# A norm's weight row spread over the partitions: products with one row of weights, or with 128 rows of which one is not zero

## The chip, the cores and the metric

The kernel runs on one core of a Trainium2 chip. The metric is the device time of one execution in microseconds. The kernel before took 1679.24 us, the median of 3 runs (1679.14 to 1679.53).

## What is computed

One inference step of a decoder trunk with one layer, for a prompt of 1024 tokens and for 8 samples of 8 tokens (64 rows), at a width of 1024. The layer begins with a norm and one large projection:

```python
def rms_norm(x, g):
    xf = x.astype(jnp.float32)
    y = xf * lax.rsqrt(jnp.mean(xf * xf, axis=-1, keepdims=True) + EPS)
    return (y * g.astype(jnp.float32)).astype(x.dtype)

h = rms_norm(x, g_pre_mix)
cb, cc, ch, q, k, v, ga, gb = jnp.split(h @ w_in, IN_SPLITS, axis=-1)
```

After that come a short gated convolution, stick-breaking attention, the output projection, a convolutional feed-forward part and an embedding gate, each with norms of its own. The change concerns only how `g_pre_mix`, the weight of the first norm (1024 values), gets onto all partitions.

## The kernel before, in words

The 1088 rows of x are held as nine blocks of at most 128 rows (`xn`, and `xlast` for the samples), with a row of x on a partition. Each block b goes through the same steps before the first projection can use it:

1. SyncE loads it (`x_start`, line 687). SyncE's order at the start is x blocks 0 and 1, the weights of job 0 (`raw`, line 655), x block 2, `g_mix` (the norm's weight, broadcast to 128 partitions by a DMA of 512 KB, line 683), x blocks 3 and 4, the weights of job 1, x blocks 5 to 8, the biases and the page table. Then it waits for the page table's landing before it loads keys, and it loads the weights of job 2 behind the first keys.
2. ScalarE squares it and sums (`x0_square`, line 1227), and takes a root as exp(-0.5 ln) (`x0_root`, lines 1232 and 1233).
3. VectorE improves the root by a Newton step (`x0_newton`, lines 1985 to 1991) and multiplies the block by the root and by the norm's weight (`x0_scaled`, line 2008).
4. TensorE transposes it in eight parts of 128x128 (`x0_turn`, through the helper `turned`, line 2794).
5. ScalarE writes the high part of the transposed block (`x0_high`, line 1240), VectorE the rest (`x0_low`, line 2016). Each product of the projection is made of three: high by high, low by high, high by low.

For a part of the weights (a "job") ScalarE makes the high part `wh` (`whi`, line 1196); for jobs 0 and 1 GpSimd subtracts it to get `wl` (line 1074), and VectorE passes the word on (`wlo_by_pool`); from job 2 on VectorE subtracts itself (line 1963).

The weight row in step 3 comes from two places. For blocks 2 to 8 it is `g_mix`, which the DMA has spread. For blocks 0 and 1 that DMA would be waited for, so the row is loaded alone (`grow`, one row of 4 KB, on ScalarE's queue, line 1217) and TensorE spreads it: a product of `ones`, one row of 128 ones that VectorE sets (line 1971), with `grow`, one row of 1024, into `pairs[0]` in two halves of 512 columns (line 2933; each fp32 product is two records in the trace). `x0_scaled` for blocks 0 and 1 waits for `p_mix`, the second product's count.

TensorE's order at the start is written out by hand in `pair` of the TensorE program (lines 2928 on). `idle(i)` issues filler transposes of the identity, `WARM = (8, 4, 11, 5, 6)` of them:

```python
idle(4)
pe.wait_ge(d_ones, 1)
pe.wait_ge(row_in, 16)
...
idle(0)
x0_turn(0)
idle(1)
x0_turn(1)
idle(2)
begin_job()
by_blocks()
```

`by_blocks` makes the first tile of 384 columns in two parts: the columns of block 0 (8 steps of three products, lines 2869 to 2871, with `x0_turn(2)` after the fourth step), then `idle(3)` and the columns of blocks 1 and 2. Then come the other tiles of jobs 0 and 1 with the turns of the later blocks between them (`in_tile`, lines 2840 to 2842), job 2, and the rest of the kernel.

GpSimd begins with the identity (lines 1042, 1043; TensorE waits for it before its first transpose), then makes masks and cleared tiles one after the other (lines 1046 to 1071), then `wl` of jobs 0 and 1. VectorE begins with `ones`, a small tile `xst` and two cleared halves of `kl` (lines 1971 to 1975) before the first Newton step.

Of the kernel before, what the change touches and what calls it, by code (L numbers as in the profile page):

```python
# [12 lines left out]
P = 128  # L13
D = 1024
# [178 lines left out]
def build(nc, inp, out, gate_spill, x1_spill, x2_spill, f_spill):  # L193
    with ExitStack() as ctx:
        def sem(name):
            return ctx.enter_context(nc.semaphore(name))
# [30 lines left out]
        a = Region(R1, R2)  # L227
# [8 lines left out]
        a = Region(R1, R2)  # L236
# [20 lines left out]
        a = Region(R3, RTOP)  # L257
# [23 lines left out]
        a = Region(R2 + ACTS, R3)  # L281
# [34 lines left out]
        aas, xs = a2.take("aas", [P, P]), a2.take("xs", [P, P])  # L316
        a = Region(start_at, start_at + 20480)
        xlast, g_mix = a.take("xlast", [P, D]), a.take("g_mix", [P, D])
        grow, ones = a.take("grow", [1, D]), a.take("ones", [1, P])
        junk0 = a.take("junk0", [P, 512]).bitcast(mybir.dt.bfloat16)  # L320
        xst = a.take("xst", [P, 48])
        farh = a.take("farh", [P, 2, NB, NT])
# [2 lines left out]
        a = Region(R3T, RTOP)  # L325
# [5 lines left out]
        a = Region(R3T, RTOP)  # L331
# [4 lines left out]
        a = Region(R3T, RTOP)  # L336
# [29 lines left out]
        a = Region(R3T, RTOP)  # L366
# [119 lines left out]
        g_const = sem("g_const")  # L486
# [18 lines left out]
        row_in, d_ones, p_mix = sem("row_in"), sem("d_ones"), sem("p_mix")  # L505
# [12 lines left out]
        a_gh = sem("a_gh")  # L518
        a_fold, d_fold, a_pack = sem("a_fold"), sem("d_fold"), sem("a_pack")
        a_sum, d_sum = sem("a_sum"), sem("g_wlo_d_sum")  # L520
        g_wlo, SUM0 = d_sum, 2

        d_lo = sem("d_lo")
        d_unit = sem("d_unit")
# [509 lines left out]
        def _(pool):  # L1034
            me = Count()

            def then(ins):
                ins.then_inc(g_self, 1)
                pool.wait_ge(g_self, me.step())

            g = nc.gpsimd
            then(g.memset(ident[:, :], 0.0))
            g.affine_select(out=ident[:, :], in_=ident[:, :], compare_op=ALU.not_equal, fill=1.0, base=0,
                            pattern=[[-1, P]], channel_multiplier=1).then_inc(g_const, 1)

            then(g.memset(far[:, :], 0.0))
            g.affine_select(out=far[:, :], in_=far[:, :], compare_op=ALU.is_gt, fill=-BIG, base=0,
                            pattern=[[-1, P]], channel_multiplier=1).then_inc(g_const, 1)
# [121 lines left out]
        def _(act):  # L1170
            s_ = nc.scalar
            me = Count()
            job, unit, mis = Count(), Count(), Count()
# [39 lines left out]
            def tables(name):  # L1213

                s_.preload_act_table_set(name)

            act.dma_start(grow[:, :], inp["g_pre_mix"]).then_inc(row_in, 16)
            tables("natural_log_exp_and_others")

            def x0(b):  # L1220
# [729 lines left out]
        def _(dve):  # L1950
            v = nc.vector
            me = Count()
            job, unit, xhn = Count(), Count(), Count()

            def then(ins):
                ins.then_inc(d_self, 1)
                dve.wait_ge(d_self, me.step())
# [10 lines left out]
                dve.wait_ge(p_unit, unit.step())  # L1968
                return unit_bank(u)[:, 0:GROUPS[gr][1]]

            v.memset(ones[:, :], 1.0).then_inc(d_ones, 1)
            then(v.memset(xst[:, :], 1.0))
            v.memset(xst[:, 40:41], EPS).then_inc(d_eps, 1)
            for h in range(2):
# [1 line left out]

            def wlo_by_pool():

                dve.wait_ge(g_wlo, job.step())
                dve.sem_inc(d_lo, 1)  # L1980

            def x0_newton(b, n):
# [765 lines left out]
        def _(pe):  # L2748
            t_ = nc.tensor
            job, unit, mis, att = Count(), Count(), Count(), Count()  # L2750
# [24 lines left out]
            def begin_job():  # L2775
                pe.wait_ge(d_lo, job.step())
# [21 lines left out]
            def x0_turn(b):  # L2798

                r = block_rows(b)  # L2800
                pe.wait_ge(d_x0, b + 1)
                if b >= 3:
                    pe.wait_ge(d_x0l, 2 * (b - (3 if b < 8 else 2) + 1))
                x = xn[:, b, :] if b < BLK else xlast[0:NS, :]
                for k in range(KD):
                    ins = turned(x0_pair(b)[:, k * P:k * P + r], x[:, k * P:(k + 1) * P], r)
                    if k % 4 == 3:
                        ins.then_inc(p_x0, 1)

            def pair(c):  # L2810
# [35 lines left out]
                def in_tile(j, gr, between={}):  # L2846
                    b = open_unit(j, gr)
                    for k in range(KD):
                        for what, n in between.get(k, ()):
                            what(n)  # L2850
                        step(b, j, gr, k)

                def idle(i):
                    for _ in range(WARM[i]):
                        turned(banks[1 if i in (2, 3) else 7][:, 0:P], ident[:, :])

                def by_blocks():

                    b = open_unit(0, 0)
                    for at_, end in ((0, P), (P, 3 * P)):  # L2860
                        if at_:
                            idle(3)
                        pe.wait_ge(d_x0l, 2 * (end // P))
                        o, cols = b[:, at_:end], slice(at_, end)
                        for k in range(KD):
                            if not at_ and k == KH:
                                x0_turn(2)
                            (h, l), xhi, xlo = tall(0, k), xh[:, k, cols], xl[:, k, cols]
                            t_.matmul(o, h, xhi, start=(k == 0), stop=False, skip_group_check=True)
                            t_.matmul(o, h, xlo, start=False, stop=False, skip_group_check=True)  # L2870
                            ins = t_.matmul(o, l, xhi, start=False, stop=(k == KD - 1), skip_group_check=True)
                    ins.then_inc(p_unit, 1)
# [8 lines left out]
                def conv_rows():  # L2881

                    b = once()
                    pe.wait_ge(cwr_in, cwn.step(32))
                    pe.sem_inc(pe_held, 1)
                    turned(b[:, 0:P], cwr[:, :]).then_inc(p_m, 1)
# [39 lines left out]

                if first:
                    idle(4)
                    pe.wait_ge(d_ones, 1)
                    pe.wait_ge(row_in, 16)  # L2930
                    for i in range(2):

                        ins = t_.matmul(banks[i], ones[:, :], grow[:, 512 * i:512 * i + 512], start=True, stop=True)
                    ins.then_inc(p_mix, 1)
# [8 lines that stand above are left out]
                    in_tile(1, 0, {1: [(x0_turn, 3)], 3: [(x0_turn, 4)], 5: [(x0_turn, 5)]})  # L2943
                    pe.wait_ge(d_x0l, 12)
                    conv_rows()
                    in_tile(0, 1, {6: [(x0_turn, 6)]})
                    past(0)
                    in_tile(1, 1, {1: [(x0_turn, 7)], 3: [(x0_turn, 8)]})
                    pe.wait_ge(d_x0l, 2 * NBK)
                    past(1)  # L2950
                    in_tile(0, 2)
                    in_tile(1, 2, {4: [(pages, 0), (past, 2)]})
                else:
                    conv_rows()
                    begin_job()
                    for gr in range(NG):
                        in_tile(0, gr)
                    past(0)
                    begin_job()
                    in_tile(1, 0)  # L2960
                    past(1)
                    in_tile(1, 1)
                    in_tile(1, 2, {4: [(pages, 0), (past, 2)]})
# [534 lines left out]
```

## Time and profile before

| | before |
|---|---|
| median of 3 runs | 1679.24 us |
| the profiled execution's own time | 1680.04 us |
| its span (first to last instruction) | 1678.3 us |
| TensorE matmul busy | 1667.5 us, 99% |
| VectorE busy | 1101.4 us, 66% |
| ScalarE busy | 794.6 us, 47% |
| GpSimd busy | 321.0 us, 19% |
| TensorE in the chain that ended last | 94% |

The profile is of one execution; its times count from the first instruction. "Busy" is the share of the span in which an engine had an instruction in work. The chain is followed back from the last instruction, at each step to what released it. PE is TensorE's matmul, PEld its weight load, DVE VectorE, ACT ScalarE, POOL GpSimd, SP SyncE; a q behind a name means the engine's instruction queue. Instructions are named by their line in the kernel.

### The profile page before, as it was taken

What the parts mean: (1) busy time and instruction counts of PE and PEld (TensorE: products, weight loads), DVE (VectorE), ACT (ScalarE), POOL (GpSimd) and SP (SyncE); (2) the same over time, 40 slices, a digit from 0 to 9 for tenths busy, and PEclk for the clock granted to TensorE, in tenths of its full rate; (3) what the DMA queues carried; (4) which work ended last, traced back from release to release, by engine and by line L of the source; (5) the groups of instructions that cost most, each with busy time, mean ns of one, the idle gap of its engine ahead of it and who ended that gap; (6) DMA issues with size and microseconds to landing.
All of it is one profiled execution on the core that took longest, in us unless ns stands there. A gap on an engine that the chain in (4) does not pass through costs nothing.

```text
span 1678.3 us, 27174 instructions
## 1 busy us (share of the span) xinstructions
PE 1667.5 (99%) x9101; PEld 1462.9 (87%) x9101; DVE 1101.4 (66%) x1606; ACT 794.6 (47%) x1391; POOL 321.0 (19%) x268
## 2 busy tenths in 40 slices
PE   9999999999999999999999999999999999999998
PEld 8999998999999999988888888888888878888886
DVE  7365246325533646547688888888888688776576
ACT  7345344444534453125454444444444444465675
POOL 2000000000000000002346666666664000000000
PEclk9999999999999999999999999999999999999999
DMA  5312221132123114443132222222222852245333
GB/s 182 97 55 74 80 77 55 57 99 68 60 67 92 53 63 149 151 169 116 68 97 80 79 79 79 79 72 72 79 79 97 293 191 80 90 150 186 112 123 118
DMA packets 176598, 170.64 MB, mean 102 GB/s; under 512 B 16207, under 2 KB 144555, under 8 KB 176492
## 3 DMA queue, kind: packets, MB, share of 16 engines
q1 hardware_dynamic: 165546, 164.41, 30.5%
q10 hardware_dynamic: 10946, 4.91, 1.0%
q8 instruction: 55, 0.90, 0.2%
q14 instruction: 51, 0.42, 0.1%
HBM read 129.66 MB, written 39.62 MB: 101 GB/s over the span
## 4 chain that ended last, share of the span: by engine, by line
PE 94%; DVE 3%; DMA 1%; issue 1%; SPq 1%; ACT 0%; DVEq 0%; POOL 0%; POOLq 0%; ACTq 0%
PE pair L3152 11%; PE pair L2840 9%; PE pair L2842 9%; PE pair L2841 9%; PE pair L3212 8%; PE pair L3214 8%; PE pair L3213 8%; PE pair L2794 6%; PE pair L3368 3%; PE pair L3370 3%; PE pair L3369 3%; PE pair L3221 3%; PE pair L3021 2%; PE pair L2771 2%; PE pair L2769 2%; PE pair L2770 2%
## 5 line engine op out<-in xcount | busy, mean ns | idle before, releaser
L2840 PE MATMUL pair<-xh,wh 128*128 128x384 f32 (+1 forms) x952 | 324.4, 341 | 0.0
L2842 PE MATMUL pair<-xh,wl 128*128 128x384 f32 (+1 forms) x952 | 311.3, 327 | 0.0
L2841 PE MATMUL pair<-xl,wh 128*128 128x384 f32 (+1 forms) x952 | 310.8, 326 | 0.0
L2840 PEld LDWEIGHTS pair<-xh,wh 128*128 128x128 f32 x952 | 179.3, 188 | 5.4 <-issue 4.0
L2841 PEld LDWEIGHTS pair<-xl,wh 128*128 128x128 f32 x952 | 179.4, 188 | 0.0
L2842 PEld LDWEIGHTS pair<-xh,wl 128*128 128x128 f32 x952 | 178.8, 188 | 0.0
L1074 POOL TENSOR_TENSOR srow<-hn,hn 128x512 f32<-128x512 f32 x8 | 12.0, 1506 | 791.1 <-DVE hn L2322 790.8
L3368 PE MATMUL pair<-woph,foph 128*128 128x512 f32 x308 | 120.9, 393 | 0.1
L3370 PE MATMUL pair<-woph,fopl 128*128 128x512 f32 x308 | 120.0, 390 | 0.0
L3369 PE MATMUL pair<-wopl,foph 128*128 128x512 f32 x308 | 120.0, 390 | 0.0
L1408 ACT ACTIVATE keep<-pair,bias 128x512 f32<-128x512 f32 (+4 forms) x100 | 58.2, 582 | 115.6 <-DVE pair L2175 71.5
L1963 DVE TENSOR_TENSOR wl<-raw,wh 128x1024 fp32r<-128x1024 f32 x46 | 56.3, 1225 | 73.9 <-ACT wh L1196 73.4
L1764 ACT ACTIVATE foph<-f 128x512 fp32r<-128x512 f32 x77 | 48.3, 628 | 71.7 <-PE pair L3370 68.3
L2175 DVE TENSOR_TENSOR pair<-pair,far 128x128 f32<-128x128 f32 x64 | 16.3, 296 | 81.7 <-PE pair L2996 59.6
L3368 PEld LDWEIGHTS pair<-woph,foph 128*128 128x128 f32 x308 | 57.8, 188 | 13.8 <-issue 1.3
L3370 PEld LDWEIGHTS pair<-woph,fopl 128*128 128x128 f32 x308 | 57.8, 188 | 12.1
L3369 PEld LDWEIGHTS pair<-wopl,foph 128*128 128x128 f32 x308 | 57.9, 188 | 11.7
L3212 PE MATMUL pair<-bh,tch 128*128 128x512 f32 x168 | 67.4, 401 | 0.0
L3214 PE MATMUL pair<-bh,tcl 128*128 128x512 f32 x168 | 65.7, 391 | 0.0
L3213 PE MATMUL pair<-bl,tch 128*128 128x512 f32 x168 | 65.5, 390 | 0.0
L3212 PE MATMUL pair<-bh,adh 128*128 128x512 f32 x168 | 65.5, 390 | 0.0
L3214 PE MATMUL pair<-bh,adl 128*128 128x512 f32 x168 | 65.4, 389 | 0.0
(417 smaller groups left out, 4289.5 us busy)
## 6 DMA issues: line engine op xcount, KB each, us to landing
rawp<-in_w_up SPq DMA_DIRECT2D x88, 256.0 KB, 3.8
raw<-in_w_in SPq DMA_DIRECT2D x80, 256.0 KB, 3.2
wd<-in_w_down SPq DMA_DIRECT2D x55, 256.0 KB, 3.0
f_spill<-cv SPq DMA_DIRECT2D x22, 552.0 KB, 2.8
f<-f_spill SPq DMA_DIRECT2D x44, 256.0 KB, 5.6
gat<-gate_spill SPq DMA_DIRECT2D x16, 544.0 KB, 4.5
x_spill<-x SPq DMA_DIRECT2D x16, 512.0 KB, 3.0
gate_spill<-stg SPq DMA_DIRECT2D x32, 192.0 KB, 1.9
```

Source lines behind the costliest of these rows:

```text
L1408: s_.activation(keep[n % 2][:, 4 * P - w:4 * P], b, ACT.Sigmoid, scale=-SCALE, bias=bias2[:, h + 2:h + 3] if n != SAMPLE else bias2[:, 5:6 ...
L2794: return t_.transpose(b, src, ident[0:rows, 0:rows])
L2840: t_.matmul(b, h, xhi, start=(k == 0), stop=False, skip_group_check=True)
L2841: t_.matmul(b, h, xlo, start=False, stop=False, skip_group_check=True)
L2842: ins = t_.matmul(b, l, xhi, start=False, stop=(k == KD - 1), skip_group_check=True)
L3152: ins = t_.matmul(o[:, 512 * c:512 * c + 512], x, w(t, c), start=first and i == 0, stop=last and i == 2, skip_group_check=True)
L3212: t_.matmul(o, w, x, start=n in "1675" and k == 0, stop=False, skip_group_check=True)
L3213: t_.matmul(o, w, xlow, start=False, stop=False, skip_group_check=True)
L3214: ins = t_.matmul(o, wlow, x, start=False, stop=k == KH - 1, skip_group_check=True)
L3368: t_.matmul(o, xh_[:, cols], w[0][:, :], start=n in (0, 2, 3, 5) and k == 0, stop=False, skip_group_check=True)
L3369: t_.matmul(o, xh_[:, cols], w[1][:, :], start=False, stop=False, skip_group_check=True)
L3370: ins = t_.matmul(o, xl_[:, cols], w[0][:, :], start=False, stop=k == KF - 1, skip_group_check=True)
```

## The change

`grow` and `ones` become tiles of 128 rows. The DMA fills 32 rows of `grow`, each with the same 1024 weights (128 KB instead of 4 KB); GpSimd clears rows 32 to 63, between the identity and its next mask, and VectorE rows 64 to 127. Of `ones` all rows are cleared and row 0 is set to one. The product is thus the same sum, with 127 terms of zero. TensorE waits for VectorE's second count and for GpSimd's, as well as for the DMA. GpSimd's count is the first of a semaphore that also counts `wl` of jobs 0 and 1 and, at the kernel's end, two sums, so these counts move up by one.

```diff
-        grow, ones = a.take("grow", [1, D]), a.take("ones", [1, P])
+        grow, ones = a.take("grow", [P, D]), a.take("ones", [P, P])
...
-        g_wlo, SUM0 = d_sum, 2
+        g_grow, SUM0 = d_sum, 3
+        g_wlo, WLO0 = d_sum, 1
...
             g.affine_select(out=ident[:, :], in_=ident[:, :], compare_op=ALU.not_equal, fill=1.0, base=0,
                             pattern=[[-1, P]], channel_multiplier=1).then_inc(g_const, 1)
 
+            pool.wait_ge(g_const, 1)
+            g.memset(grow[32:64, :], 0.0).then_inc(g_grow, 1)
+            pool.wait_ge(g_grow, 1)
             then(g.memset(far[:, :], 0.0))
...
-            act.dma_start(grow[:, :], inp["g_pre_mix"]).then_inc(row_in, 16)
+            act.dma_start(grow[0:32, :], inp["g_pre_mix"].rearrange("l d -> (l d)").partition_broadcast(32)).then_inc(row_in, 16)
             tables("natural_log_exp_and_others")
...
-            v.memset(ones[:, :], 1.0).then_inc(d_ones, 1)
+            then(v.memset(ones[:, :], 0.0))
+            v.memset(ones[0:1, :], 1.0).then_inc(d_ones, 1)
+            v.memset(grow[64:P, :], 0.0).then_inc(d_ones, 1)
             then(v.memset(xst[:, :], 1.0))
...
-                dve.wait_ge(g_wlo, job.step())
+                dve.wait_ge(g_wlo, WLO0 + job.step())
...
                     idle(4)
-                    pe.wait_ge(d_ones, 1)
+                    pe.wait_ge(d_ones, 2)
+                    pe.wait_ge(g_grow, 1)
                     pe.wait_ge(row_in, 16)
```

## Rows read from the trace of the kernel before

**Rows 1.** The page: shares of the chain that ended last, by engine
```profile
...
PE 94%; DVE 3%; DMA 1%; issue 1%; SPq 1%; ACT 0%; DVEq 0%; POOL 0%; POOLq 0%; ACTq 0%
...
```

**Rows 2.** The chain in order of time, 0 to 60 us: start us, us, what
```profile
...
1.60 1.54 PE pair L2794 x6
3.14 3.71 PE pair L2933 x4
6.85 7.05 PE pair L2794 x39
...
```

**Rows 3.** Source line L2794 (transposes) in two windows: duration ns min/median/max, first and last start
```profile
...
L2794 PE MATMUL pair<-ident x7: 421/421/475, 6.8 to 8.1; 128*128 128x128 f32 x7
...
L2794 PE MATMUL pair<-ident x10: 272/272/273, 12.5 to 13.5; 128*128 128x128 f32 x10
L2794 PE MATMUL pair<-ident,xn x3: 272/273/317, 12.2 to 12.4; 128*128 128x128 f32 x3
...
```

**Rows 4.** Timeline of the entry: start us, us, engine line op out<-in; weight loads of the products
```profile
...
4.09 0.33 PEld L2933 LDWEIGHTS pair<-grow,ones 1*128 1x128 f32 x1 [0.52 <-issue]
...
4.94 0.33 PEld L2933 LDWEIGHTS pair<-grow,ones 1*128 1x128 f32 x1 [0.52 <-issue]
...
```

**Rows 5.** The same timeline, from x block 0 to the weights of job 1
```profile
...
4.63 1.06 ACT L1227 ACTIVATE junk<-xn 128x1024 bf16<-128x1024 f32 x1 [1.96 <-DMA xn<-in_x_prompt]
...
6.37 0.15 DVE L1985 TENSOR_SCALAR xst<-xst 128x1 f32<-128x1 f32 x1 [2.78 <-ACT xst L1233]
...
6.87 0.16 DVE L1991 SCALAR_TENSOR_TENSOR xst<-xst 128x1 f32<-128x1 f32 x1
7.06 1.28 DVE L2008 SCALAR_TENSOR_TENSOR xn<-xn,xst,pair 128x1024 f32<-128x1024 f32 x1
...
8.95 1.28 DVE L2008 SCALAR_TENSOR_TENSOR xn<-xn,xst,pair 128x1024 f32<-128x1024 f32 x1
9.07 2.38 POOL L1074 TENSOR_TENSOR wl<-raw,wh 128x1024 fp32r<-128x1024 f32 x1 [1.00 <-ACT wh L1196]
9.21 1.06 ACT L1227 ACTIVATE junk<-xn 128x1024 bf16<-128x1024 f32 x1 [0.23 <-DMA xn<-in_x_prompt]
...
10.40 1.09 ACT L1240 ACTIVATE xh<-pair 128x512 fp32r<-128x512 f32 x2
...
11.03 1.29 DVE L2016 TENSOR_TENSOR xl<-pair,xh 128x512 fp32r<-128x512 f32 x2 [0.80 <-ACT xh L1240]
...
12.92 1.28 DVE L2008 SCALAR_TENSOR_TENSOR xn<-xn,xst,g_mix 128x1024 f32<-128x1024 f32 x1
...
13.66 0.31 PE L2869 MATMUL pair<-xh,wh 128*128 128x128 f32 x1
...
15.04 1.06 PE L2794 MATMUL pair<-ident,xn 128*128 128x128 f32 x8
15.70 1.08 ACT L1240 ACTIVATE xh<-pair 128x512 fp32r<-128x512 f32 x2 [0.76 <-PE pair L2794]
...
17.80 2.40 POOL L1074 TENSOR_TENSOR wl<-raw,wh 128x1024 fp32r<-128x1024 f32 x1 [6.35 <-ACT wh L1196]
...
```

**Rows 6.** SyncE's longest wait before 80 us, and the loads by stretch (last column GB/s)
```profile
...
SPq L643 <- DMA pgt<-in_page_table: 8.3, 1, 8.3
...
4.00:18.50 14.50, 14.50 (x86) 12.34 (x85) 10.02 (x21) 12.32 (x25) 6.67 (x17) 1.00 1.05 368
...
```

**Rows 7.** Timeline around the first use of the weights of job 2
```profile
...
46.37 1.21 DVE L1963 TENSOR_TENSOR wl<-raw,wh 128x1024 fp32r<-128x1024 f32 x1
...
49.15 0.34 PE L2840 MATMUL pair<-xh,wh 128*128 128x384 f32 x1
...
```

**Rows 8.** GpSimd's memsets, groups by line, engine and form
```profile
...
L1070 POOL MEMSET qpad<- 128x1152 f32 x1 | 1.1, 1057 | 0.0
...
```

**Rows 9.** TensorE and its granted clock (PEclk is the third figure) at the end of the span
```profile
...
1671.60:1674.50 2.90, 0.00 (x0) 1.00 0.01 3
1674.50:1678.30 3.80, 0.00 (x0) 0.50 0.37 138
...
```

## The prediction

> **What bounds the kernel now.** I read the page first: TensorE is busy nearly throughout, and the chain that ended last is 94% TensorE [rows 1]. The change touches only the entry, so the question is narrow: by how much does it move the moment from which TensorE works without a break, and is anything later tied to an absolute time? The chain in order of time answers for the entry [rows 2]: transposes and four one-row products follow each other on TensorE until 13.9 us, then the chain passes through ScalarE, VectorE and back while the first blocks of x are normed, turned and split. From 30 us on it is TensorE nearly alone.
>
> The second thing to see is TensorE's own pace. The page's clock line reads 9 from the first slice, but before 12.2 us it has no record of the clock; the instructions tell more. Transposes of 128x128 start 213 ns apart at 7 us (x7, first to last 6.8 to 8.1) and 109 ns apart at 13 us (x10, 12.5 to 13.5), with 421 and 272 ns for one [rows 3]. That factor of two is the step from 1.2 to 2.4 GHz, and it falls at 12.2 us, where a 317 ns transpose stands between both kinds [rows 3]. TensorE had had no gap since 1.60 [rows 2]. So it ran 10.6 us at the low clock though it was always occupied. In the first part of that time it did six transposes, then four products with one active row (the form 1*128, 3.14 to 6.85), and from then on only transposes with 128 rows [rows 2, 4]. The likeliest reading: products with one active row don't raise the clock, and the rise came 12.2 - 6.85, about 5.4 us, after the last of them. The change makes exactly these four full-height.
>
> **The change, part by part.**
> The products. Still two fp32 products of 512 columns in four records, the last ones 0.85 us apart (loads at 4.09 and 4.94 [rows 4]), which is 4 x 213 ns for 4 x 128 columns: the pace goes by columns, the same for 1 row [rows 4] and 128 rows [rows 3]. So 128 rows cost nothing per se. No column is added.
>
> The clock. Now all TensorE work from 1.60 on has 128 rows. If the rise keeps the distance that it had to the end of the one-row work, it comes at 1.60 + 5.4 = 7.0 us; it may come earlier, while the products run, which would then end up to 1.7 us sooner (four at 0.43 instead of 0.85). Where it falls between 5 and 10 us makes no difference to what follows, as (a) and (b) show.
>
> What that gives, step by step, with warm transposes at 0.109 instead of 0.213 us. (a) The spread weight row is wanted by the first scaling (L2008) at 7.06, right behind VectorE's own Newton steps, whose last ends at 6.87 + 0.16 = 7.03 [rows 5]; the products end at 6.85. An earlier row is worth nothing there: late next are the Newton steps, behind ScalarE and the landing of x block 0. (b) x0_turn(0) follows the end of the scaling, 8.34, and takes 0.9 instead of 1.7 us, but ScalarE can't take it before 10.40, when it is through with the square of block 2, whose block landed at 9.21 [rows 5]. Nothing again. (c) x0_turn(1), the 11 filler transposes and the first product at 13.66 [rows 5]: warm, turn 1 would begin when scaling 1 is done, 8.95 + 1.28 = 10.23, end at 11.2, the fillers end at 12.4, and the first product would wait for xl of block 0, ready at 11.03 + 1.29 = 12.32. So it starts 1.2 us earlier. (d) Twelve products later TensorE needs block 2 scaled. That ends at 12.92 + 1.28 = 14.20, while turn 2 started at 15.04 [rows 5]. The path takes 15.04 - 14.20 less 0.05 to 0.2 of hand-over: **0.65 to 0.8 us saved**, and the other 0.4 of the 1.2 becomes a new wait of TensorE for VectorE at about 14. (e) Behind that, the next steps hang on turn 2: ScalarE's split at 15.70 waited for TensorE; VectorE's split and TensorE's second part follow it, and so do the weights of job 1, whose low part GpSimd makes from 17.80 to 20.20 when ScalarE has made the high one [rows 5]. They all shift together, so the gain is kept. I also looked for something fixed in time that would eat it. SyncE waits 8.3 us for the page table's DMA [rows 6] and loads keys and the weights of job 2 behind that, but VectorE has split those at 46.37 + 1.21 = 47.6 and TensorE's tile with them begins at 49.15 [rows 7]: 1.5 us of slack, beside a gain below 1. From there to the end TensorE is the bound, and a gain at the entry arrives whole.
>
> The larger DMA. One row of 4 KB becomes 32 rows, 128 KB, on ScalarE's queue at 0.81, beside SyncE's first block of x. All loads from 4 to 18.5 us run at 368 GB/s [rows 6], which is their limit here. The added 127 KB are 0.34 us of that, so every later landing moves by 0 (if they fit in before the stream is full) to 0.34 us. x block 0 (4.63) and block 2 (9.21) are both waits for a landing and both on the path of (d) [rows 5]. I take the upper end, since the copy shares its first microsecond with block 0: **0.34 lost**. The row itself must be there when TensorE is through with its six transposes at 3.14 [rows 2]. I expect 2.5 to 3.6 us, from block 0's own 128 rows of 4 KB, which took until 4.6; at worst the products end 0.5 later, 7.3 cold, 0.3 behind the Newton steps, which would add to the 0.34 only if the clock stays low.
>
> GpSimd. One memset of 32x1024. A memset of 1152 columns took it 1057 ns [rows 8], so about 0.95 us for 1024, if the time goes by columns, and with the waits before and behind it 1.2 us. It starts when the mask is done that also releases TensorE at 1.60 [rows 2] and ends near 1.6 + 0.1 + 0.95 = 2.65, before 3.14. Everything behind it on GpSimd comes 1.2 us later: the last of its constants ended at 9.07 - 1.00 = 8.07 [rows 5], now 9.3; then wl of job 0, before at 9.07, starts 0.2 late and ends at 11.7, wanted by TensorE at 12.4 at the earliest. Cover is 0.7 us; without it the 0.2 would count.
>
> VectorE. Two small memsets and a self wait in place of one, and 64x1024 of zeros: by GpSimd's rate again 0.95, in all 1.3 us more. Begun near 0.9 that ends near 2.5, before TensorE asks. What follows on VectorE ends 1.3 late, and it was idle for 2.78 us before 6.37 [rows 5]. Nothing. The added waits on TensorE stand in front of the products alone. Renumbered counts cost nothing, and no tile moves, since a one-row tile took 4096 bytes of each partition before as well.
>
> **Sum:** -0.75 + 0.34 = -0.4 us (ends: -0.8 and -0.35 with the clock early). The profiled execution lasted 1680.04, of which 1678.3 are the span; 0.4 less is 1679.64. The median of the three runs is 0.80 below that execution, which puts the forecast at 1679.24 - 0.4 = **1678.8**. It is 0.02%; a measurement of this kernel tells about 0.2% (3.4 us) from no change, so this is "the same".
>
> **The rivals.**
> (1) Clock unmoved. The 127 added rows are zeros, and the one-row form may not be the reason for the late rise. For it: only one rise is recorded, so the cause is inferred. Against: the transposes that did precede the rise read the identity, 127 zeros of 128. Then only the DMA's 0.34 is left: 1679.6. Worked through the cold path, the weight row may come at 7.3 and add 0.3: 1679.9.
> The Trainium skill, "TensorE: Matmul & The Clock Gate", Part 1, lets sustained busy time open the gate and does not mention active rows. By it this rival would hold; the trace speaks against it, with 10.6 us of unbroken work at the low clock.
>
> (2) Slower: the clock rises early and falls again. With the products over by 5.9 and the 8 fillers warm, TensorE rests from about 6.8 to 8.7, where before it had no gap, and again near 10. If the clock falls there and the next rise comes 5.4 us after the rest, it is near 14: turn 0 from 8.7, fillers and turn 1 cold until 13.0, four more fillers cold, seven warm, end at 14.6 against 13.63 before. That is +0.95: 1680.2. Only if it stays cold past turn 2 (to about 18.5 us) does it add 1.7 for the fillers, up to 1.0 for twelve products and 0.8 for turn 2: 1682.7, and this is the point from which "slower" would begin. Against: the one fall that is recorded came near 1674.5, when TensorE had done nothing since at least 1671.6, 2.9 us [rows 9], and the rests here are below 2 us.
> [...]
>
> (3) The row or the loads come much later than thought (over 1 us): 1680.3, as each us of landing is a us on the path.
>
> **Numbers.** Early clock as forecast 0.62; rival 1 0.20; rival 2 0.12 (of it 0.02 beyond 3.4 us); rival 3 and unforeseen things 0.06. Three runs spread over 0.4 us and one profiled execution stood 0.8 above them, so I widen the ends: 1677.9 takes in the full 0.8 gain with half a us of scatter, 1680.3 takes in rivals 1 and the mild form of 2. Faster by over 0.2% would need 3.4 us, more than TensorE's entire loss to the low clock on the path: 0.01. Slower 0.03, same 0.96.
>
> **What would show it.** Transposes 109 ns apart already in x0_turn(0) or (1) and a record of the clock that begins before 8 us; gaps on TensorE at 7 to 8.4 and about 10; first product near 12.7; turn 2 near 14.7; everything after it 0.4 earlier. The landing of block 0 at 4.9 and of block 2 at 9.5 would show the DMA's price. Transposes still 213 ns apart at 11 us would mean rival 1, a return to 213 after 109 rival 2.

## The result, and the profile after

The changed kernel takes 1681.98 us in the median of 22 runs (1680.45 to 1682.66), the kernel before 1679.42 in 22 runs beside them (1678.73 to 1680.31). The medians are 2.6 us apart. The ratio of the runs is 1.0013, with a 95% interval of 1.0008 to 1.0019: slower, and outside the forecast's range of 1677.9 to 1680.3. It is less than the 0.2% that the text took as the bound of what can be told; with 22 runs of each it can be told. (Of all runs told of here one, of e7, took 1830.12 us in a slow state of the chip; it is left out of e7's median.)

The page of the changed kernel: the span, the busy time and the chain's shares, which stand against 1678.3 us and the 94% of [rows 1].

```profile
span 1680.1 us, 27177 instructions
...
PE 1665.8 (99%) x9101; PEld 1461.0 (87%) x9101; DVE 1104.3 (66%) x1608; ACT 795.0 (47%) x1391; POOL 321.2 (19%) x269
...
PE 93%; DVE 4%; SPq 1%; DMA 1%; issue 1%; ACT 0%; DVEq 0%; ACTq 0%
...
```

TensorE is busy 1.7 us less and the span is 1.8 us longer. So TensorE stands idle 3.5 us more than before, and its work in the entry takes less time, because more of it runs at the high clock. The timeline of the entry shows where (start us, us, engine line); it answers to [rows 2, 4, 5], with line numbers shifted by the change (2933 is now 2940, 2008 is 2014, 1991 is 1997).

```profile
...
1.61 0.94 POOL L1048 MEMSET grow<- 32x1024 f32 x1
...
4.71 3.75 PE L2940 MATMUL pair<-grow,ones 128*128 128x512 f32 x4 [1.57 <-DMA grow<-in_g_pre_mix]
...
5.30 1.06 ACT L1231 ACTIVATE junk<-xn 128x1024 bf16<-128x1024 f32 x1 [2.74 <-DMA xn<-in_x_prompt]
...
8.59 1.28 DVE L2014 SCALAR_TENSOR_TENSOR xn<-xn,xst,pair 128x1024 f32<-128x1024 f32 x1 [0.90 <-PE pair L2940]
...
9.61 1.06 ACT L1231 ACTIVATE junk<-xn 128x1024 bf16<-128x1024 f32 x1
9.64 2.37 POOL L1078 TENSOR_TENSOR wl<-raw,wh 128x1024 fp32r<-128x1024 f32 x1 [0.43 <-ACT wh L1200]
...
9.97 0.27 DVE L1993 TENSOR_SCALAR xst<-xst 128x1 f32<-128x1 f32 x1
10.28 1.74 DVE L1997 SCALAR_TENSOR_TENSOR xst<-xst 128x1 f32<-128x1 f32 x1
...
12.05 1.28 DVE L2014 SCALAR_TENSOR_TENSOR xn<-xn,xst,pair 128x1024 f32<-128x1024 f32 x1
...
13.39 1.10 PE L2800 MATMUL pair<-ident,xn 128*128 128x128 f32 x8 [1.89 <-DVE xn L2014]
...
15.44 0.30 PE L2875 MATMUL pair<-xh,wh 128*128 128x128 f32 x1
...
16.82 1.06 PE L2800 MATMUL pair<-ident,xn 128*128 128x128 f32 x8
...
```

The waits of the first 40 us name the two new ones (us in total, times, longest):

```profile
...
PE pair L2940 <- DMA grow<-in_g_pre_mix: 1.6, 1, 1.6
...
DVE xn L2014 <- PE pair L2940: 0.9, 1, 0.9
...
```

Read from the top. GpSimd's memset took 0.94 us, as forecast. TensorE was through with its six transposes at 3.14 as before, but the products start at 4.71, not 3.14: the copy of 32 rows landed only then. Block 0 of x landed at 5.30, not 4.63. The first scaling starts at 8.59 instead of 7.06, after 0.9 us of waiting for the products. So far the delay is 1.5 us. Then comes something that the forecast had not seen: VectorE's last Newton step for block 1, an instruction on 128x1 elements that takes 0.16 us, takes **1.74 us**. It starts at 10.28, while GpSimd's subtraction for job 0 runs from 9.64 to 12.01, and it ends when that ends. In the kernel before, the same step ran at 8.75, GpSimd began at 9.07 [rows 5], and the second scaling at 8.95. The step for block 3, though, was held in that kernel too, inside GpSimd's second subtraction. Both stand in the timeline of the kernel before:

```profile
...
8.75 0.16 DVE L1991 SCALAR_TENSOR_TENSOR xst<-xst 128x1 f32<-128x1 f32 x1
...
18.02 2.21 DVE L1991 SCALAR_TENSOR_TENSOR xst<-xst 128x1 f32<-128x1 f32 x1
...
```

In the change the second scaling starts at 12.05, 3.1 us late, and turn 1 at 13.39 instead of 11.1.

Part of it is taken back, because turn 1 now runs wholly at the high clock: 1.10 us instead of 1.60. The transposes by duration (min/median/max ns, first and last start), which answer to [rows 3]:

```profile
...
L2800 PE MATMUL pair<-ident x12: 272/421/421, 8.3 to 11.2; 128*128 128x128 f32 x12
...
L2800 PE MATMUL pair<-ident,xn x8: 272/272/338, 10.0 to 10.8; 128*128 128x128 f32 x8
...
```

The step from 421 to 272 ns falls at about 10.1, where a 338 ns transpose opens turn 0, against 12.2 before. Turn 1 at 13.39 lies behind either. The eleven fillers behind turn 1 take 1.36 us in both kernels. The first product starts at 15.44 (13.66 before) and turn 2 at 16.82 (15.04 before): **+1.78 us**. From there these two executions stay together: the last product starts at 1672.97 against 1671.24, +1.73, and their times, 1681.77 and 1680.04, differ by 1.73.

### The profile page after: what moved, and what is told of

It is laid out like the page before. It is cut to its first block, busy times and chain, and to the rows that moved or that the text cites. A ratio compares the mean times of both kernels' runs of the same rounds, so it can differ in the third digit from the quotient of the medians.

```text
span 1680.1 us, 27177 instructions
## 1 busy us (share of the span) xinstructions
PE 1665.8 (99%) x9101; PEld 1461.0 (87%) x9101; DVE 1104.3 (66%) x1608; ACT 795.0 (47%) x1391; POOL 321.2 (19%) x269
## 4 chain that ended last, share of the span: by engine, by line
PE 93%; DVE 4%; SPq 1%; DMA 1%; issue 1%; ACT 0%; DVEq 0%; ACTq 0%
PE pair L3159 11%; PE pair L2846 9%; PE pair L2848 9%; PE pair L2847 9%; PE pair L3219 8%; PE pair L3221 8%; PE pair L3220 8%; PE pair L2800 5%; PE pair L3375 3%; PE pair L3376 3%; PE pair L3377 3%; PE pair L3228 3%; PE pair L3028 2%; PE pair L2777 2%; PE pair L2775 2%; PE pair L2776 2%
## 5 line engine op out<-in xcount | busy, mean ns | idle before, releaser
L3377 PEld LDWEIGHTS pair<-woph,fopl 128*128 128x128 f32 x308 | 57.8, 188 | 12.2
```

The source lines that it names most:

```text
L3377: ins = t_.matmul(o, xl_[:, cols], w[0][:, :], start=False, stop=k == KF - 1, skip_group_check=True)
```

## The experiments

Each experiment is told as a difference from the kernel before or from the change. The time beside each is the median of 11 runs (22 for the change), and that of the kernel before over the runs made beside them (22 to 35). The landmark is the start of turn 2 in the profiled execution. From there to the end ten of the thirteen profiled executions took 1664.9 to 1665.3 us. The others took 1663.9 (e6), 1663.6 (e11) and 1666.1 (e8). In e6 and e8 most of that difference is TensorE's idle time between 1200 and 1400 us, 0.1 and 1.7 us against 0.8 before; why it differs was not looked into, nor e11's. The products start at 3.07 in the timeline, which counts them from the first record, and at 3.14 in the chain [rows 2].

| kernel | median us | before us | 95% interval of the ratio | products start | turn 2 starts |
|---|---|---|---|---|---|
| before | | | | 3.07 | 15.04 |
| the change | 1681.98 | 1679.42 | 1.0008 to 1.0019 | 4.71 | 16.82 |
| e1, only the copy to 32 rows | 1681.82 | 1679.61 | 1.0006 to 1.0024 | 4.67 | 16.78 |
| e2, 128 rows, copy of one row after clearing | 1681.83 | 1679.61 | 1.0004 to 1.0022 | 6.61 | 17.13 |
| e3, change, subtraction after the Newton steps | 1680.35 | 1679.61 | 0.9995 to 1.0013 | 4.71 | 15.23 |
| e4, change, GpSimd clears nothing | 1681.99 | 1679.61 | 1.0006 to 1.0024 | 4.66 | 16.77 |
| e6, before, one filler more | 1679.84 | 1679.59 | 0.9992 to 1.0010 | 3.29 | 14.39 |
| e7, before, four fillers more | 1681.29 | 1679.59 | 1.0005 to 1.0022 | 3.93 | 16.21 |
| e8, change, copy to 64 rows | 1683.38 | 1679.59 | 1.0012 to 1.0029 | 6.44 | 17.67 |
| e10, before, 128-row products on zeros | 1679.08 | 1679.59 | 0.9991 to 1.0008 | 2.94 | 14.24 |
| e12, before, an extra copy behind the row's | 1680.17 | 1679.63 | 0.9995 to 1.0013 | 3.07 | 15.24 |
| e9, before, job 1's low part by VectorE | 1678.34 | 1679.63 | 0.9984 to 1.0002 | 3.08 | 14.37 |
| e11, change, with e3's and e9's edits | 1679.21 | 1679.63 | 0.9990 to 1.0008 | 4.80 | 15.03 |

The theory: the copy of 32 rows lands late, and that lateness pushes a VectorE step behind GpSimd's subtraction, where it is held. The text calls this the cliff: a small delay is free, a little more sets off a large one. The rivals: the later landings of x alone (A), harm by the early clock (B), GpSimd's own delay (C), a delay that passes through one to one (D).

### The copy alone (e1)

```diff
-        grow, ones = a.take("grow", [1, D]), a.take("ones", [1, P])
+        grow, ones = a.take("grow", [P, D]), a.take("ones", [1, P])
...
-            act.dma_start(grow[:, :], inp["g_pre_mix"]).then_inc(row_in, 16)
+            act.dma_start(grow[0:32, :], inp["g_pre_mix"].rearrange("l d -> (l d)").partition_broadcast(32)).then_inc(row_in, 16)
...
-                        ins = t_.matmul(banks[i], ones[:, :], grow[:, 512 * i:512 * i + 512], start=True, stop=True)
+                        ins = t_.matmul(banks[i], ones[:, :], grow[0:1, 512 * i:512 * i + 512], start=True, stop=True)
```

> The kernel before with one part of the change: the DMA brings the weight row to 32 partitions, and the products still read one row. Theory (the copy of 32 rows lands late, and the delay makes VectorE's last Newton step of block 1 wait behind GpSimd's subtraction for job 0): the copy lands near 4.7 us, the products run 4.7 to 8.4, the first scaling ends near 9.9, the Newton step of block 1 takes about 1.7 us instead of 0.16, and turn 2 starts at 16.8 to 17.5 (15.04 before). Time 1.8 to 2.7 us above before. The clock rises later than in the kernel before, near 13.8, if one-row products don't raise it. Rival A (the loads of x are what counts, 0.34 to 0.7 us each): time 0.3 to 0.7 above before, turn 2 near 15.6. Rival B (the early clock of the change is what harms): time as before, within 0.3.

The timeline of e1: the products, the first scaling, the subtraction, the held step, turn 2.

```profile
...
4.67 3.75 PE L2933 MATMUL pair<-grow,ones 1*128 1x512 f32 x4 [1.53 <-DMA grow<-in_g_pre_mix]
...
8.55 1.28 DVE L2008 SCALAR_TENSOR_TENSOR xn<-xn,xst,pair 128x1024 f32<-128x1024 f32 x1 [0.89 <-PE pair L2933]
...
9.61 2.37 POOL L1074 TENSOR_TENSOR wl<-raw,wh 128x1024 fp32r<-128x1024 f32 x1 [1.53 <-ACT wh L1196]
...
10.24 1.75 DVE L1991 SCALAR_TENSOR_TENSOR xst<-xst 128x1 f32<-128x1 f32 x1
...
16.78 1.06 PE L2794 MATMUL pair<-ident,xn 128*128 128x128 f32 x8
...
```

The time is 2.2 us above before, and turn 2 starts within 0.04 of the change's. As far as the intervals tell, the copy alone makes the whole loss; the 128-row form, the memsets and the added waits make no difference that shows. Rivals A and B, as the whole cause, fall with the same run. One point of the expectation was missed: the clock rose at about 11.1, not 13.8, though the one-row products ended at 8.35 here.

### GpSimd's memset (e4)

```diff
...
-            pool.wait_ge(g_const, 1)
-            g.memset(grow[32:64, :], 0.0).then_inc(g_grow, 1)
-            pool.wait_ge(g_grow, 1)
...
-            v.memset(grow[64:P, :], 0.0).then_inc(d_ones, 1)
+            v.memset(grow[64:P, :], 0.0)
+            v.memset(grow[32:64, :], 0.0).then_inc(d_ones, 1)
...
-                    pe.wait_ge(g_grow, 1)
```

> The change with GpSimd's memset moved to VectorE, which clears rows 32 to 63 behind rows 64 to 127. Theory: GpSimd's constants end 1.2 us earlier, but its subtraction waits for ScalarE at 9.6 either way, and VectorE is done before the copy of 32 rows lands at 4.7: time within 0.3 us of the change's, turn 2 at 16.8. Rival C (GpSimd's delay is what costs): 1 us or more below the change's.

The time is 1681.99, and turn 2 starts at 16.77. Rival C falls: GpSimd's subtraction starts at 9.60 here and at 9.64 in the change, since both wait for ScalarE's high part.

### The hold taken away (e3)

```diff
                 pool.wait_ge(a_hi, j + 1)
+                if j == 0:
+                    pool.wait_ge(d_self, 8)
```

The count `d_self` reaches 8 when VectorE is through with the Newton steps of block 1.

> The change as it is, with one wait more: GpSimd starts its subtraction for job 0 only when VectorE is through with the Newton steps of block 1. Theory: that last step takes 0.16 instead of 1.74 us, the second scaling starts near 10.5 instead of 12.05, turn 2 starts at 15.0 to 15.4 instead of 16.82, and the time is 1.4 to 1.8 us below the change's, near before. Rival A (late loads and the late row alone make the 1.8 us): no more than 0.3 below the change's.

```profile
...
10.28 0.16 DVE L1999 SCALAR_TENSOR_TENSOR xst<-xst 128x1 f32<-128x1 f32 x1
10.47 1.28 DVE L2016 SCALAR_TENSOR_TENSOR xn<-xn,xst,pair 128x1024 f32<-128x1024 f32 x1
...
10.59 2.38 POOL L1078 TENSOR_TENSOR wl<-raw,wh 128x1024 fp32r<-128x1024 f32 x1 [1.40 <-DVE xst L1999]
...
15.23 1.06 PE L2802 MATMUL pair<-ident,xn 128*128 128x128 f32 x8
...
```

The step takes 0.16 again and the second scaling follows at 10.47. One wait **added** to GpSimd, which now starts its subtraction 0.95 later, brings turn 2 from 16.82 to 15.23 and the time from 1681.98 to 1680.35. The products start as late as in the change. Turn 2 is within 0.19 of the profiled execution of before, but that one had a late clock. Against e6 and e9, which have the rows and the copy of the kernel before and a clock that rose near 10.7 and 10.6 (turn 2 at 14.39 and 14.37), e3's turn 2 is still 0.85 late. So the held step is 1.6 us of the loss, and the rest, below 1 us, is something else (see "The base").

### A late row without any change to a DMA (e6, e7)

```diff
-WARM = (8, 4, 11, 5, 6)
+WARM = (8, 4, 11, 5, 7)
```

and the same with 10 in place of 7: fillers ahead of the one-row products.

> The kernel before with 7 filler transposes instead of 6 ahead of the one-row products; the DMA is as before. It makes the spread row 0.2 us later and nothing else. Theory (a cliff: the Newton step of block 1 must start before GpSimd's subtraction at 9.07, it had 0.3 us to spare): the step starts near 8.8 to 8.9 and takes 0.16; turn 2 within 0.2 of 15.04, the time as before within 0.3.

```profile
...
8.88 0.16 DVE L1991 SCALAR_TENSOR_TENSOR xst<-xst 128x1 f32<-128x1 f32 x1
8.96 2.38 POOL L1074 TENSOR_TENSOR wl<-raw,wh 128x1024 fp32r<-128x1024 f32 x1 [0.89 <-ACT wh L1196]
...
14.39 1.06 PE L2794 MATMUL pair<-ident,xn 128*128 128x128 f32 x8
...
```

> The kernel before with 10 fillers instead of 6: the spread row comes 0.85 us later (near 7.7), with no change to any DMA and with one-row products. Theory (the cliff): the Newton step of block 1 starts near 9.5, behind GpSimd's start at 9.07, and is held until 11.45, so the second scaling starts near 11.5 instead of 8.95 (2.5 later for a row 0.85 later), turn 2 starts at 16.0 to 16.4, the time is 1.0 to 1.4 above before. Rival A (the landings of x are what counts) and rival D (a delay passes through one to one): turn 2 at most 0.85 later, time at most 0.85 above before, the Newton step 0.16.

```profile
...
9.04 2.36 POOL L1074 TENSOR_TENSOR wl<-raw,wh 128x1024 fp32r<-128x1024 f32 x1 [0.94 <-ACT wh L1196]
...
9.52 1.89 DVE L1991 SCALAR_TENSOR_TENSOR xst<-xst 128x1 f32<-128x1 f32 x1
...
11.45 1.28 DVE L2008 SCALAR_TENSOR_TENSOR xn<-xn,xst,pair 128x1024 f32<-128x1024 f32 x1
...
16.21 1.06 PE L2794 MATMUL pair<-ident,xn 128*128 128x128 f32 x8
...
```

With one filler more the step starts at 8.88, GpSimd at 8.96, and the step takes 0.16. With four more it starts at 9.52, behind GpSimd's 9.04, and takes 1.89. A row later by 0.85 us makes the second scaling 2.5 us later (11.45 against 8.95) and turn 2 1.2 us later than in the profiled execution of before (1.8 later than in e6). The time is 1.7 above before, more than the 1.0 to 1.4 that was expected. That is the cliff, made without touching a copy or a product. Rivals A and D fall as the whole cause. (Turn 2 of e6 is even earlier than before, at 14.39 instead of the expected 15.04: its clock rose near 10.7; see below.)

### Later loads with the row on time (e12)

```diff
-            hold(page_in, 16)
+            hold(page_in, 32)
...
             act.dma_start(grow[:, :], inp["g_pre_mix"]).then_inc(row_in, 16)
+            act.dma_start(pv[0:32, 0:8, :].rearrange("p a b -> p (a b)"), inp["g_pre_mix"].rearrange("l d -> (l d)").partition_broadcast(32)).then_inc(page_in, 16)
```

The added copy counts on the semaphore for which SyncE waits before it loads keys, so that wait goes from 16 to 32.

> The kernel before with its one-row copy first on ScalarE's queue and a second copy of 32 rows behind it, into a tile that nobody reads (it is added traffic only). The row is on time, the loads of x are delayed as in the change. Theory (it is the row's lateness that trips the cliff, not x's): block 0 lands near 5.2 (4.6 before), the products still end near 6.85, the Newton step of block 1 takes 0.16, turn 2 starts at 15.0 to 15.6 (less if the clock rises before 11), time 0 to 0.6 above before. Rival A (x's delay is what costs): 1.5 or more above before.

```profile
...
5.06 1.06 ACT L1228 ACTIVATE junk<-xn 128x1024 bf16<-128x1024 f32 x1 [2.01 <-DMA xn<-in_x_prompt]
...
9.40 0.16 DVE L1992 SCALAR_TENSOR_TENSOR xst<-xst 128x1 f32<-128x1 f32 x1
...
10.06 2.37 POOL L1074 TENSOR_TENSOR wl<-raw,wh 128x1024 fp32r<-128x1024 f32 x1 [1.99 <-ACT wh L1196]
...
15.24 0.86 PEld L2795 LDWEIGHTS pair<-ident,xn 128*128 128x128 f32 x8 [0.40 <-DVE xn L2009]
...
```

Block 0 landed at 5.06, and the Newton step at 9.40 is not held, because the same later loads also delay GpSimd, to 10.06. Turn 2 starts at 15.24, and the time is 0.5 above before, which the interval doesn't tell from nothing. The clock rose near 10.0 here, with one-row products. Against e6 and e9, which have a like clock, turn 2 is 0.85 later: the later loads move it, through block 2's scaling, for which TensorE waits. So the traffic has a price of its own, below 1 us; it is the row's own lateness that trips the cliff.

### How late a copy lands (e8, e2)

e8 is the change with `grow[0:64]` and a broadcast to 64 in the copy, and GpSimd's memset left out.

> The change with the suspected cost doubled: the DMA brings the row to 64 rows (256 KB), GpSimd clears nothing. Theory (the copy competes with the first block of x and both land later in proportion): the copy lands near 5.5 us (4.7 with 32 rows), block 0 near 5.8 (5.3), turn 2 near 17.2, time 0.3 to 0.8 above the change's. Because GpSimd holds VectorE until 12.0 in any case, the 0.8 of the row comes through only in part. If the copy's price is a fixed one: 4.7 and the change's time.

The products in e8 (ns min/median/max, first and last start), and TensorE's wait for the copy (us, times):

```profile
...
L2936 PE MATMUL pair<-grow,ones x4: 967/1061/1192, 6.4 to 9.1; 128*128 128x512 f32 x4
...
  DMA grow<-in_g_pre_mix: 3.3, 1
...
```

The timeline of e8, for block 0 and the held step:

```profile
...
5.32 1.06 ACT L1228 ACTIVATE junk<-xn 128x1024 bf16<-128x1024 f32 x1 [2.61 <-DMA xn<-in_x_prompt]
...
11.92 0.96 DVE L1994 SCALAR_TENSOR_TENSOR xst<-xst 128x1 f32<-128x1 f32 x1
...
```

With 32 rows more the products start 1.7 us later (6.44 against 4.71), twice what was expected, and the time is 1.4 above the change's, where 0.3 to 0.8 was expected. Block 0 of x did not land later than in the change (5.32 against 5.30), so the theory of a delay in proportion for both failed. The step was held for a shorter time, since the row came so late that GpSimd was well into its subtraction.

e2 has the change's products, but VectorE clears the whole tile first and the copy brings one row. GpSimd's memset and TensorE's wait for it are left out, as in e4:

```diff
...
-            act.dma_start(grow[0:32, :], inp["g_pre_mix"].rearrange("l d -> (l d)").partition_broadcast(32)).then_inc(row_in, 16)
+            act.wait_ge(d_ones, 1)
+            act.dma_start(grow[0:1, :], inp["g_pre_mix"]).then_inc(row_in, 16)
...
+            v.memset(grow[:, :], 0.0).then_inc(d_ones, 1)
             then(v.memset(ones[:, :], 0.0))
             v.memset(ones[0:1, :], 1.0).then_inc(d_ones, 1)
-            v.memset(grow[64:P, :], 0.0).then_inc(d_ones, 1)
```

> The change with its DMA undone: VectorE clears the whole tile of 128 rows first (one memset), then the DMA brings one row of 4 KB; the products have 128 rows. Nothing is cleared by GpSimd. Theory: the row lands near 3.4 us, the products follow at once, the clock rises before 10 us, the Newton step of block 1 ends before GpSimd's subtraction begins (9.07) if the first scaling starts before 7.3, and turn 2 starts at 14.4 to 14.9. Time 0.2 to 0.7 us below before. If the first scaling starts later than 7.3, the Newton step is held and turn 2 comes after 16: time 1 to 1.5 above before. Rival B (an early clock falls again or harms): time above before by 1 or more although the Newton step isn't held. Rival A: as before within 0.2.

```profile
...
2.04 0.53 ACTq L1219 DMA_DIRECT2D grow<-in_g_pre_mix  x1
...
4.57 1.06 ACT L1229 ACTIVATE junk<-xn 128x1024 bf16<-128x1024 f32 x1 [0.67 <-DMA xn<-in_x_prompt]
...
6.61 3.75 PE L2937 MATMUL pair<-grow,ones 128*128 128x512 f32 x4 [3.47 <-DMA grow<-in_g_pre_mix]
...
8.98 2.36 POOL L1075 TENSOR_TENSOR wl<-raw,wh 128x1024 fp32r<-128x1024 f32 x1 [0.89 <-ACT wh L1197]
...
12.18 0.16 DVE L1995 SCALAR_TENSOR_TENSOR xst<-xst 128x1 f32<-128x1 f32 x1
...
```

This was meant to be the better version, and it failed on a term that I had taken for granted. A copy of 4 KB issued at 2.04 let the products start only at 6.61, 4.6 us later; the same copy issued at 0.81 let them start at 3.07, when TensorE was free. x's block 0 landed at 4.57 as ever. What differs is the moment: at 0.81 nothing is in flight, at 2.04 SyncE's loads of x are ahead of it. That these loads are the reason is the likeliest reading; no run separates it from another. The time is 2.2 above before, and not by the cliff. The expectation had the Newton step held if the row came late; here the row was so late that the step, at 12.18, came behind the whole of GpSimd's subtraction (8.98 to 11.34) and took 0.16. The row's own delay of 3.5 us is what moved turn 2 to 17.13.

### The clock alone (e10)

```diff
...
-            act.dma_start(grow[:, :], inp["g_pre_mix"]).then_inc(row_in, 16)
+            act.dma_start(pv[0:1, 0:8, :].rearrange("p a b -> p (a b)"), inp["g_pre_mix"]).then_inc(row_in, 16)
...
-            v.memset(ones[:, :], 1.0).then_inc(d_ones, 1)
+            then(v.memset(ones[:, :], 0.0))
+            v.memset(ones[0:1, :], 1.0).then_inc(d_ones, 1)
+            v.memset(grow[:, :], 0.0).then_inc(d_ones, 1)
...
-                    pe.wait_ge(d_ones, 1)
+                    pe.wait_ge(d_ones, 2)
```

> The products with 128 rows at the time they had before: they read a cleared tile of 128 rows, so the norm's weight is left out for blocks 0 and 1 (it comes out as zero); the row's DMA of 4 KB stays, into a tile that isn't used. TensorE works without a gap from 1.6 us, always with 128 rows. It tests the clock alone. Theory (one-row products don't raise the clock, 128-row ones do): the clock rises by 7.0, the products end by 6.9 or sooner, turn 2 starts at 14.3 to 14.5, the time is 0.5 to 0.8 below before. If the one-row form is not the reason: the clock rises near 12 as before, turn 2 at 15.04. If it falls again in the rests at 7 and 10: turn 2 after 15.

```profile
...
1.60 1.54 PE L2796 MATMUL pair<-ident 128*128 128x128 f32 x6 [1.60 <-POOL ident L1043]
2.94 2.58 PE L2935 MATMUL pair<-grow,ones 128*128 128x512 f32 x4
5.36 1.04 PE L2796 MATMUL pair<-ident 128*128 128x128 f32 x8
...
14.24 0.86 PEld L2796 LDWEIGHTS pair<-ident,xn 128*128 128x128 f32 x8 [0.41 <-DVE xn L2010]
...
```

The product records of e10 (ns min/median/max, first and last start):

```profile
...
L2935 PE MATMUL pair<-grow,ones x4: 592/732/1061, 2.9 to 4.9; 128*128 128x512 f32 x4
...
```

The four products take 2.58 us instead of 3.78, and the eight fillers from 5.36 on are at the high clock (8 in 1.04 us). The second product record, started at 3.8, lasts 871 ns, between the 1061 of the first and the 592 or 593 of the last two, so the rise falls between 3.8 and 4.5. It is one execution, but in none of the six profiled ones with one-row products did the clock rise before 10.0. TensorE rested from 6.4 to 8.5 after that and its clock did not fall back (turn 0, from 8.49, takes 1.09 us). Turn 2 starts at 14.24, 0.80 before the profiled execution of before. The medians differ by 0.5 us, which the interval doesn't tell from nothing.

### The other hold taken away (e9, e11)

Before and after alike, VectorE's Newton step of block 3 is held by GpSimd's second subtraction (2.21 us at 18.02 before, for 0.16 us of work). e9 lets VectorE make that low part itself:

```diff
-        g_wlo, SUM0 = d_sum, 2
+        g_wlo, SUM0 = d_sum, 1
...
-            for j in range(2):
+            for j in range(1):
                 pool.wait_ge(a_hi, j + 1)
...
                     x0_scaled(3, 1, 4)
-                    wlo_by_pool()
+                    wlo()
```

> The kernel before, with the low part of the weights of job 1 made by VectorE (1.22 us) right behind the third scaling, where GpSimd made it (2.4 us) and held VectorE's Newton step of block 3 for 2.21 us meanwhile. Theory (what GpSimd holds is on the path): the Newton step takes 0.16, block 3 is scaled by 19.6 instead of 21.5, the 0.26 us wait of TensorE at 21.6 and the 0.7 us one at 28.9 vanish, time 0.5 to 1.0 below before. If the hold is off the path: time as before, within 0.3.

VectorE in e9, and turn 2:

```profile
...
17.39 0.16 DVE L1991 SCALAR_TENSOR_TENSOR xst<-xst 128x1 f32<-128x1 f32 x1
...
18.78 1.22 DVE L1963 TENSOR_TENSOR wl<-raw,wh 128x1024 fp32r<-128x1024 f32 x1
...
14.37 0.86 PEld L2794 LDWEIGHTS pair<-ident,xn 128*128 128x128 f32 x8
...
```

The step takes 0.16 and the subtraction 1.22. Block 3 is scaled by 18.9. Of TensorE's two waits that were to vanish, the first is gone and the second is down from 0.7 to 0.3 us. 1678.34 is the lowest median of all kernels here, 1.3 below before, but the interval of the ratio (0.9984 to 1.0002) includes no change: that e9 is faster is likely and not shown.

> The change with the wait of e3 (GpSimd's subtraction for job 0 behind the Newton steps of block 1) and with the low part of job 1 made by VectorE. Theory: the two savings add: 1.4 to 1.8 and 0.5 to 1.0 below the change's, about 0.5 below before, and about as fast as the kernel before with only the second.

The time is 1679.21, 2.8 below the change and 0.4 below before. With both holds gone the change costs 0.9 against e9, which has the old products and the old copy; the expectation had them about equal. So no version that was run shows a gain by the 128-row product with its copy.

## Why the prediction was wrong, point by point

**The product's cost.** Right: 128 rows take as long as one. The last records are 0.85 us apart in both forms, and turn 2 starts at 16.78 in e1 and at 16.82 in the change.

**The landing of the row: the first step that failed.** "I expect 2.5 to 3.6 us ... at worst the products end 0.5 later." The products could start only at 4.7, and they ended 1.6 later. I had priced the copy by its bytes in a full stream (0.34 us), and its landing by a guess next to block 0's. In this place 31 rows more cost 1.6 us of waiting (4.71 against 3.07), and 32 more on top of them 1.7 (e8).

**x's landings.** Mis-sized: block 0 came 0.67 later, not 0.34 (5.30 against 4.63). In e12, where the loads alone are late, turn 2 is 0.85 later than in e6 and e9, and the median 0.5 above before, which its interval doesn't tell from nothing.

**How a delay goes on: the step that decided.** The text let each delay of the row pass through one to one, in the DMA's part ("0.3 behind the Newton steps, which would add to the 0.34") and in rival 3 ("each us of landing is a us on the path"). Rival 3 had the place, and 0.06 for itself together with everything unforeseen; it had no mechanism. What the runs show is a threshold: the Newton step of block 1 ran at 8.75, 0.3 us before GpSimd's subtraction at 9.07. A row 0.2 later costs nothing that shows (e6), one 0.85 later costs 1.7 us (e7), and the change loses 1.6 us of its 2.6 to that one held instruction (e3). The warning stood in the same trace: the same line took 2.21 us at 18.02, inside GpSimd's second subtraction. I took that stretch as steps of which "They all shift together" and did not ask which other overlap it could make.

The Trainium skill, "SBUF — State Buffer", section "Who interferes with whom", has the rule: a VectorE instruction with two inputs in SBUF and a GpSimd instruction that reads SBUF exclude each other, and the one that starts first keeps the other out to its end. The trace agrees: the steps with one tensor input ran beside the subtraction at their usual length (0.27 us at 9.97), the step with two inputs, 0.16 us by itself, took 1.74.

**The clock.** Half right. The rise did come earlier, 10.1 instead of 12.2, but not by 7.0. TensorE stood still from 3.14 to 4.71; whether that is why, no run shows. Nor does the 10.1 show that the rows did it: with the change's products it came between 8.0 (e11) and 10.7 (e2), with one-row products between 10.0 (e12) and 12.2 (before). Only e10, at 3.8 to 4.5, stands clear of both. That the rise keeps a distance of 5.4 us to the end of the one-row work was no rule: it came 5.4 us after their end in the kernel before, 3.2 after it in e12 and 2.7 after it in e1. And its worth was overrated. In the change it decides nothing: e1, with a rise 1.0 later, has the same turn 2, because the held scaling comes later than either. Even alone and earliest (e10), it gives 0.80 at turn 2 against the one profiled execution of before, but only 0.15 against e6 and e9, which have one-row products and a turn 2 at 14.39 and 14.37.

**What is late next.** Right as far as it went: with an early clock and the row on time, turn 2 starts right behind a wait for block 2's scaling (e10, e12).

**GpSimd's and VectorE's memsets.** Right: they take 0.94 and 0.91 us and are hidden, as e4 shows for GpSimd's.

**The base.** The change costs 1.73 between the two profiled executions and 2.56 between the medians. Up to turn 2, e9 is the kernel before, and yet its turn 2 came at 14.37 where the profile of before had 15.04, with a clock that rose near 10.6 instead of 12.2. So the profile that I worked from had a late rise, and lay 0.62 above its median (1680.04 against 1679.42); the change's lay 0.21 below its own. These two make up the other 0.83. The saving of 0.65 to 0.8 us in step (d) was taken from that late rise, and e6 and e9 had most of it with the old products and the old copy. Measured against their turn 2, the change is 2.4 us late, near the 2.6 of the medians. Of that the held step is 1.6 (e3). The other 0.85 remains in e3; the late row and the late loads share it, and no run divides it, though e12 shows that the loads alone can make as much. That the rise moves about from one execution to the next is seen in the profiles; its share in the medians was not measured.

**Rivals 1 and 2.** Rival 2 did not occur: the clock did not fall back, and in e10 it held through two microseconds of rest. Rival 1 can't be ruled out for the change itself, as its rise lies within what one-row products gave too. Two sums were off without weight in the forecast: the lower saving is 0.65 - 0.34 = 0.31, not 0.35, and rival 2's 1682.7 holds its 3.5 us of cold work without the 0.95 before them.

## What to carry to other kernels

Where an instruction of one engine runs just before one of another that would shut it out, note the distance between them beside the path: a delay smaller than that is free, a slightly larger one costs nearly the whole length of the other instruction (here the step took 1.74 and 1.89 us beside one of 2.37), and a still larger one less again (0.96 in e8, none in e2). Look in the trace for an instruction that takes ten times its usual length somewhere; the pair that makes it will do so again wherever a change brings the two together. And price a copy at the start of a kernel by its landing among the other loads there, not by its bytes, above all when it is issued later or made wider.

## What was not expected of the hardware

- A wait added to GpSimd (e3) made the changed kernel 1.6 us faster, by the order of two instructions on two engines.
- A 4 KB copy took 4.6 us from issue to use when issued at 2.04 us, after two loads of 0.5 MB, and at most 2.3 us when issued at 0.81 (e2 against before). Copies of 32 and 64 rows issued at 0.81 let the products start at 4.7 and 6.4.
- With 128-row work from 1.6 us without a gap the clock rose between 3.8 and 4.5 us (e10, one execution); with one-row products among the same transposes it rose between 10.0 and 12.2 (before, e1, e6, e7, e9, e12), and with 128-row products behind a gap between 8.0 and 10.7 (the change, e2, e3, e4, e8, e11). Why it varies there stays open.
